# Attention's queues reordered, with two output slabs split into an idle buffer, in a two-layer decoder trunk

## The reference

```python
# layer 0
x = x + short_conv_mixer(rms_norm(x, a_norm), a_w_in, a_conv, a_w_out)
x = x + squared_relu_mlp(rms_norm(x, mlp_norm[0]), w_up[0], w_down[0])
k, v = shared_kv(x, kv_norm, w_kv, k_norm)
# layer 1: 8 heads, each with two score maps c = 0, 1 (64 features each) and 128 value features
q  = rms_norm_per_head((rms_norm(x, b_norm) @ w_q), q_norm)
for i in range(4):                                  # query blocks of 128 tokens
    sc = einsum('bqhcd,bkhcd->bhcqk', q_i, k[:128*(i+1)]) * 64**-0.5
    p  = softmax(where(causal, sc, -1e30))
    a  = p[:, :, 0] - lam * p[:, :, 1]
    o_i = einsum('bhqk,bkhe->bqhe', a, v[:128*(i+1)])
x = x + (rms_norm(o, sub_norm) * (1 - lam_init)) @ w_o
x = x + squared_relu_mlp(rms_norm(x, mlp_norm[1]), w_up[1], w_down[1])
```

## Time and profile before

| what | value |
|---|---|
| median of 3 runs | 1116.61 us (1116.53 to 1118.18) |
| the profiled execution's own time | 1118.27 us |
| its span, first to last instruction | 1116.5 us |
| busy, share of the span | PE 98%, PEld 81%, DVE 71%, ACT 43%, POOL 7% |
| mean granted TensorE clock | 0.998 of full speed |
| from the first query projection's end to the last output slab's first wait | about 631 to 758 us |

### The profile page before, as it was taken

The page is one execution under the profiler, slowest core; times in us unless marked ns, Lnnn a source line. Parts: engine busy times, 40 slices in busy tenths (PEclk is TensorE's granted clock), DMA queues, the critical chain, the costliest instruction groups (busy, mean ns, idle before and its releaser), DMA issues.

```text
span 1116.5 us, 13390 instructions
## 1 busy us (share of the span) xinstructions
PE 1097.5 (98%) x5168; PEld 904.3 (81%) x5168; DVE 788.3 (71%) x980; ACT 478.8 (43%) x695; POOL 77.4 (7%) x58
## 2 busy tenths in 40 slices
PE   8999999999999999999999998899999999999998
PEld 7888888888888888888888776677888888888887
DVE  4766554787787787688754577946668678678686
ACT  6221233453353353355532466834544344344343
POOL 0000012000000000002410211013100000000000
PEclk9999999999999999999999999999999999999999
DMA  7433462315315215201322300142323423414302
GB/s 189 104 87 108 144 203 77 114 38 172 93 39 187 76 64 163 76 1 58 113 95 76 113 1 20 58 151 86 104 75 111 116 76 117 127 59 139 87 1 76
DMA packets 144751, 105.89 MB, mean 95 GB/s; under 512 B 12592, under 2 KB 121136, under 8 KB 144688
## 3 DMA queue, kind: packets, MB, share of 16 engines
q1 hardware_dynamic: 143648, 105.03, 30.8%
q10 hardware_dynamic: 1040, 0.00, 0.1%
HBM read 102.93 MB, written 2.10 MB: 94 GB/s over the span
## 4 chain that ended last, share of the span: by engine, by line
PE 94%; DVE 3%; issue 1%; ACT 1%; DMA 1%; SPq 0%; ACTq 0%; DVEq 0%
PE ps L586 31%; PE ps L613 27%; PE ps L473 19%; PE ps L675 10%; PE ps L700 2%; PE ps L761 1%; DVE nmax L1508 1%; PE ps L739 1%; DMA kv<-in_x 1%; PE ps L751 0%; PE ps L555 0%; DVE h L1544 0%; PE ps L720 0%; PE ps L568 0%; PE ps L649 0%
## 5 line engine op out<-in xcount | busy, mean ns | idle before, releaser
L586 PE MATMUL ps<-h,w_hi 128*128 128x512 f32 x1024 | 316.2, 390 | 0.0
L613 PE MATMUL ps<-w_hi,h 128*128 128x512 f32 x896 | 277.3, 389 | 0.0
L586 PEld LDWEIGHTS ps<-h,w_hi 128*128 128x128 f32 x1024 | 191.6, 188 | 39.4
L473 PE MATMUL ps<-h,w_hi 128*128 128x512 f32 x640 | 198.6, 392 | 2.0 <-DVE h L1544 1.6
L586 PE MATMUL ps<-h,w_lo 128*128 128x512 f32 x512 | 199.3, 389 | 0.0
L613 PEld LDWEIGHTS ps<-w_hi,h 128*128 128x128 f32 x896 | 168.2, 188 | 34.8
L613 PE MATMUL ps<-w_lo,h 128*128 128x512 f32 x448 | 174.3, 389 | 0.0
L931 ACT ACTIVATE w_hi<-b_raw 128x1024 fp32r<-128x1024 f32 x80 | 82.0, 1054 | 141.4 <-PE ps L586 81.9
L473 PEld LDWEIGHTS ps<-h,w_hi 128*128 128x128 f32 x640 | 118.9, 188 | 26.8 <-DVE h L1544 1.8
L473 PE MATMUL ps<-h,w_lo 128*128 128x512 f32 x320 | 124.6, 389 | 0.0
L1245 DVE TENSOR_TENSOR w_lo<-b_raw,w_hi 128x1024 fp32r<-128x1024 f32 x80 | 95.9, 1223 | 26.7 <-ACT w_hi L931 26.7
(11 more groups left out here) (132 smaller groups left out, 1190.0 us busy)
## 6 DMA issues: line engine op xcount, KB each, us to landing
b_raw<-in_w_down SPq DMA_DIRECT2D x64, 512.0 KB, 4.5
w_raw<-in_w_up SPq DMA_DIRECT2D x64, 512.0 KB, 4.0
w_raw<-in_a_w_in SPq DMA_DIRECT2D x23, 512.0 KB, 3.7
w_raw<-in_w_kv SPq DMA_DIRECT2D x16, 512.0 KB, 3.7
w_raw<-in_a_w_out SPq DMA_DIRECT2D x8, 512.0 KB, 4.0
w_raw<-in_w_q SPq DMA_DIRECT2D x8, 512.0 KB, 3.5
w_raw<-in_w_o SPq DMA_DIRECT2D x8, 512.0 KB, 4.1
kv<-in_x SPq DMA_DIRECT2D x4, 512.0 KB, 6.9
```

Source lines behind the costliest of these rows:

```text
L473: last = nc.tensor.matmul(ps[:, bank, :], w[:, s, k * P:(k + 1) * P], src(half, k), start=(k == 0 and i == 0), stop=(k == KC - 1 and i == 2))
L586: last = nc.tensor.matmul(ps[:, v % 4, :], w[:, s_, k * P:(k + 1) * P], h_of[inp][:, half, k, :], start=(k == 0 and i == 0), stop=(k == KC ...
L613: last = nc.tensor.matmul(ps[:, CHAIN[p][tb], :], op[half][:, k, tb * P:(tb + 1) * P], w[:, s_, cols], start=(FRESH[p] and k == 0 and i == ...
```

## The change

1. **PE's order.** V(n) and V(n+1) of a head stand together in its third step, V(n+2) in its fourth and V(n+3) behind T(n+4) of the next head: V(n-1), which stood ahead of T(n), now stands behind it in a head's first step. T(n+1) has no V ahead of it any more. The last third of `project` stands behind V(n+1) and `queries_T`.
2. **DVE's order.** `out_ms` is cut into `out_sums`, which now stands ahead of M(n+3), and the rest behind it. `out_norm` stands ahead of W(n+3), and `q_stats` ahead of M(n+5).
3. **ACT's order.** E(n+4), the first of the next head, stands ahead of C(n+2). The square of `copy_o` becomes `square_o`, with a semaphore of its own, behind C(n); the copy stands behind E(n+2), ahead of C(n+1).
4. **W(n).** The exponential of c = 1 comes first, and the reciprocal waits for it alone. The product of three one-column values is a `scalar_tensor_tensor` in place of a `tensor_scalar`.
5. **Slabs 0 and 1** are split into a new buffer `wo_two`, which lies where `a_raw` lies (the MLP's buffer, idle in attention), in heads 1 and 2. Slabs 2 and 3 are split in head 7, between E(29) and C(28) on ACT and behind W(29) on DVE. Slabs 4 and 5 are split ahead of `out_hi(7)`; slabs 6 and 7 and the MLP's first two are given other places among the residual additions.
6. **The end of the projection.** `out_T(7)` stands ahead of the second half of slab 3's chunks 0 to 5.
7. **Second MLP.** The first two `copy_x` stand ahead of the split and of `row_scales`.

```diff
-WO_EARLY = {(2, 3): 0, (3, 3): 1, (4, 2): 2, (5, 2): 3}
+WO_EARLY = {1: (0,), 2: (1,), 7: (2, 3)}
-WO_SPLITS = ((4, 5), (), (6,), (7,), (), (), (8,), (), (9,))
+WO_SPLITS = ((), (), (), (6,), (7,), (8,), (), (9,), ())
...
+def freed(n):
+
+    if S_WO <= n < S_WO + 6:
+        return None if n < S_WO + 2 else used(n - 4) if n < S_WO + 4 else used(n - 8)
+    return used(n - RING) if n >= RING else None
...
+        with nc.sbuf_tensor("wo_two", [P, 2, 2, SLAB], F32R) as wo_two:
+            pass
         a_raw = sb("a_raw", [P, KC, T])
...
+        def home(n, half):
+
+            if S_WO <= n < S_WO + 2:
+                return wo_two[:, n - S_WO, half, :]
+            return (w_hi, w_lo)[half][:, slot(n), :]
...
```

PE's queue:

```diff
-            for n in range(STEPS):
-                h, i = divmod(n, 4)
-                if n + 2 < STEPS:
-                    scores(n + 2)
-                if h < 3 and i < 3:
-                    project(5 + h, (range(0, 3), range(3, 6), range(6, KC))[i])
...
-                if n:
-                    values(n - 1)
-                if i == 2 and h < 4:
-                    queries_T(4 + h)
-                if i == 3 and h:
-                    out_T(h - 1)
-                weights_T(n)
+            for h in range(H):
+                n = 4 * h
+                scores(n + 2)
+                if h < 3:
+                    project(5 + h, range(0, 3))
+                weights_T(n)
+                if n:
+                    values(n - 1)
+
+                scores(n + 3)
+                if h < 3:
+                    project(5 + h, range(3, 6))
...
+                if h >= 3:
+                    project_out(0, WO_FILL[h, 1])
+                weights_T(n + 1)
+
+                if h < H - 1:
+                    scores(n + 4)
...
+                if h == H - 1:
                     pe.wait_ge(s_exp, 2 * STEPS - 2)
                     project_out(1, range(0, 3))
...
+                values(n)
+                values(n + 1)
+                if h < 4:
+                    queries_T(4 + h)
+                if h < 3:
+                    project(5 + h, range(6, KC))
+                weights_T(n + 2)
+
+                if h < H - 1:
+                    scores(n + 5)
+                if h == H - 1:
                     project_out(1, range(3, 5))
...
+                if h:
                     out_T(h - 1)
+                values(n + 2)
+                weights_T(n + 3)
...
             project_out(2, range(2, 6))
-            project_out(3, range(0, 6))
+            project_out(3, range(0, 3))
+            out_T(H - 1)
+            project_out(3, range(3, 6))
             for m in range(ACC):
                 project_out(m, range(6, 7))
-            out_T(H - 1)
...
```

ACT's queue, in the second MLP and then in attention:

```diff
+                        if new and j == 1:
+                            copy_x(0)
+                            copy_x(1)
                         if j < 6:
                             hi(q, j + 2)
...
-                        if new and j == 1:
-                            copy_x(0)
-                        if new and j:
+                        if new and j > 1:
                             copy_x(j)
...
-                for c in range(2):
+                for c in (1, 0):
...
+            def square_o(h):
+                act.wait_ge(s_pv, 4 * h + 4)
+                if h:
+                    act.wait_ge(s_oms, h)
+                nc.scalar.activation(o_sq, ps[:, B_O, :], ACT.Square).then_inc(s_osq, 1)
...
+            for h in range(H):
+                n = 4 * h
+                exps(n + 1)
+                for m in WO_EARLY.get(h, ()):
+                    split(S_WO + m)
+                evacuate(n)
+                if h:
+                    square_o(h - 1)
+
+                exps(n + 2)
+                if h:
                     copy_o(h - 1)
...
+                evacuate(n + 1)
+
+                exps(n + 3)
+                if h < 4:
                     q_hi(4 + h)
...
+                if h < H - 1:
+                    exps(n + 4)
+                evacuate(n + 2)
+
+                if h < 3:
                     take_q(5 + h)
...
+                if h:
                     out_hi(h - 1)
...
+                evacuate(n + 3)
+            square_o(H - 1)
             copy_o(H - 1)
+            split(S_WO + 4)
+            split(S_WO + 5)
             out_hi(H - 1)
...
```

DVE's queue:

```diff
-                dve.wait_ge(s_exp, 2 * m + 2)
+                dve.wait_ge(s_exp, 2 * m + 1)
                 V.reciprocal(rinv[:, b, 0:1], rsum[:, h % 2, i, 1:2]).then_inc(s_sc, 1)
                 dve.wait_ge(s_sc, 2 * m + 1)
-                V.tensor_scalar(rinv[:, b, 1:2], rinv[:, b, 0:1], rsum[:, h % 2, i, 0:1], lams[:, 5:6],
-                                ALU.mult, ALU.mult).then_inc(s_sc, 1)
+                dve.wait_ge(s_exp, 2 * m + 2)
+                V.scalar_tensor_tensor(rinv[:, b, 1:2], rinv[:, b, 0:1], lams[:, 5:6], rsum[:, h % 2, i, 0:1],
+                                       ALU.mult, ALU.mult).then_inc(s_sc, 1)
...
+            for h in range(H):
+                n = 4 * h
+                if h >= 2:
                     out_lo(h - 2)
...
+                row_max(n + 2)
+                weights(n + 1)
+                if h < 4:
+                    q_norm_part(4 + h)
+                for m in WO_EARLY.get(h, ()):
+                    split(S_WO + m)
+
+                if h:
+                    out_sums(h - 1)
+                row_max(n + 3)
+                if h:
                     out_ms(h - 1)
...
+                weights(n + 2)
+
+                if h < H - 1:
+                    row_max(n + 4)
+                if h:
                     out_norm(h - 1)
...
+                if h < 4:
                     q_lo(4 + h)
...
+                weights(n + 3)
+
+                if h < 3:
                     q_stats(5 + h)
...
+                if h < H - 1:
+                    row_max(n + 5)
+                    weights(n + 4)
             out_lo(H - 2)
+            out_sums(H - 1)
             out_ms(H - 1)
+            split(S_WO + 4)
             out_norm(H - 1)
+            split(S_WO + 5)
             out_lo(H - 1)
```

More of the change, by code:

```diff
@@ L262, in build @@
         s_oc = sem("s_oc")
+        s_osq = sem("s_osq")
         s_ost = sem("s_ost")
@@ L471, in product @@
                         wait_chunk(k)
-                    for i, (w, half) in enumerate(((w_hi, 0), (w_hi, 1), (w_lo, 0))):
-                        last = nc.tensor.matmul(ps[:, bank, :], w[:, s, k * P:(k + 1) * P], src(half, k),
+                    for i, (w, half) in enumerate(((home(n, 0), 0), (home(n, 0), 1), (home(n, 1), 0))):
+                        last = nc.tensor.matmul(ps[:, bank, :], w[:, k * P:(k + 1) * P], src(half, k),
                                                 start=(k == 0 and i == 0), stop=(k == KC - 1 and i == 2))
@@ L758, in values @@
                 if i == 0 and h:
-                    pe.wait_ge(s_oc, 2 * h)
+                    pe.wait_ge(s_osq, h)
+                    pe.wait_ge(s_oc, h)
                 for j in range(i + 1):
@@ L840, in split @@
                 act.wait_ge(s_raw[n % RAW], 16 * (raw(n) // RAW + 1))
-                if n >= RING:
-                    act.wait_ge(s_used, used(n - RING))
-                nc.scalar.activation(w_hi[:, slot(n), :], w_raw[:, n % RAW, :], ACT.Copy).then_inc(s_whi, 1)
+                if freed(n) is not None:
+                    act.wait_ge(s_used, freed(n))
+                nc.scalar.activation(home(n, 0), w_raw[:, n % RAW, :], ACT.Copy).then_inc(s_whi, 1)
             def chunk_hi(i, m, g):
@@ L1086, in copy_o @@
                     act.wait_ge(s_oT, h)
-                    act.wait_ge(s_oms, h)
                 nc.scalar.activation(o_sb, ps[:, B_O, :], ACT.Copy).then_inc(s_oc, 1)
-                nc.scalar.activation(o_sq, ps[:, B_O, :], ACT.Square).then_inc(s_oc, 1)
             def out_hi(h):
@@ L1107, in _ @@
             q_hi(3)
-            for n in range(STEPS):
-                h, i = divmod(n, 4)
-                if n + 1 < STEPS:
-                    exps(n + 1)
-                if i == 0 and h:
+            for h in range(H):
[8 more added lines that the diff above has]
+                if h:
                     copy_o(h - 1)
-                if i == 2 and h < 4:
+                evacuate(n + 1)
+                exps(n + 3)
+                if h < 4:
                     q_hi(4 + h)
-                if i == 3 and h < 3:
+                if h < H - 1:
+                    exps(n + 4)
+                evacuate(n + 2)
+                if h < 3:
                     take_q(5 + h)
-                evacuate(n)
-                if i == 3 and h:
+                if h:
                     out_hi(h - 1)
-                if (h, i) in WO_EARLY:
-                    split(S_WO + WO_EARLY[h, i])
+                evacuate(n + 3)
+            square_o(H - 1)
             copy_o(H - 1)
+            split(S_WO + 4)
+            split(S_WO + 5)
             out_hi(H - 1)
@@ L1524, in weights, with out_sums @@
```

(6 more changed lines are left out.)

26 lines of the change are left out of this document (4 added, 22 removed).

## The result

The changed kernel takes 1103.94 us (median of 4, 1103.85 to 1104.02) against 1116.65 (median of 4, 1116.53 to 1118.18); the ratio is 0.9883, 95% interval 0.9866 to 0.99. The profiled executions are 1104.02 us round a span of 1102.2, and 1118.27 round 1116.5. Their spans differ by 14.3 us, their medians by 12.7; the first experiment says why.

The account below looks back on a forecast made before the run. DVE was taken to set the pace in heads 3 to 6, with PE waiting. The terms 0.3 + 3.9 + 6.6 - 1.0 + 2.0 + 1.2 = 13.0 us, from 1116.61, gave 1103.6 us, range 1100.0 to 1109.0.

Parts of the forecast that it names:

- heads 0 to 2: First three attention heads, bound by PE: V(n+2) no longer waits for its C, 0.3 us gained (0 to 0.9).
- head 3: Attention head 3: 10.8 us against 14.69, with a late entry of DVE, 3.9 us gained (3.0 to 5.0).
- heads 4 to 6: Attention heads 4 to 6: 25.8 us in place of 32.44, 6.6 us gained (4.5 to 7.5).
- head 7: Last attention head: slab splits on ACT delay E(30) and PE waits, 1.0 us lost (0.3 to 2.5).
- the end: Behind attention: waits for the low part of chunk 7 and a weight split go, 2.0 us gained (1.5 to 2.2).
- the second MLP: Second MLP's start: PE's wait for `copy_x` goes, 1.2 us gained (0.9 to 1.2).
- the reading of the old order: Heads 3 to 6 before: DVE's turn of 8.93 us plus a 1.2 split gives 10.15, so DVE sets the pace.
- The first rival: Chains between engines set the pace: heads 4 to 6 at 9.5 each, 1107.3 us, chance 0.15; at 10.15, 1110.2, 0.08.
- The new order: A steady head laid out anew: every input comes in time, DVE sets the pace, 8.6 us a head (8.3 to 9.3).
- W's operation: W's middle operation on DVE, four a head: 152 ns in place of 273, saving 0.48 us a head.
- DVE's turn: One head's work on DVE without a slab split: falls from 8.93 to 8.45 us.
- The clock: Rival: small waits over heads 3 to 7 make PE run at 1.2 GHz, up to 1129 us; chance 0.03.

Follow-up runs that it names:

- the first experiment: The kernel before, profiled once more with no edit: 1116.63 us, span 1114.8.
- Experiment 3: The kernel before with old orders and old W operation, but slab splits and `wo_two` as in the changed kernel: 1113.58 us, ratio 0.9971.
- experiment 5: The changed kernel with `out_T` put back behind V(n+2) on PE and `out_hi` back behind C(n+3) on ACT: 1109.07 us, ratio 0.9925.
- experiments 9 and 10: Against the changed kernel: 9 adds one more reduction a head on DVE, 1107.49 us; 10 brings back W's old `tensor_scalar`, 1104.80 us.
- Experiment 11: The changed kernel with slabs 2 and 3 split later in head 7 and `q_stats` put behind W(n+4) on DVE: 1101.66 us, ratio 0.9863.
- Experiment 6: The changed kernel with V put back one step, V(n-1) ahead of T(n) and V(n) ahead of T(n+1): 1108.52 us, ratio 0.9918.
- experiment 12: The changed kernel with the last third of `project` put back ahead of V(n), V(n+1) and `queries_T`: 1106.59 us, ratio 0.9906.
- experiment 4: The changed kernel with slabs 2 and 3 split later in head 7, behind C(30) and C(31) on ACT and W(31) on DVE: 1102.83 us.
- experiments 5 to 8: Besides 5 and 6, the changed kernel with E(n+4) back behind C(n+2) on ACT (7), 1104.51 us, or `out_sums` back behind M(n+3) on DVE (8), 1105.45 us.

## Why the prediction was right, and where its reasons were not

Its time, 1103.6 us, lies 0.3 from the measured 1103.94. Term by term, forecast and then measured between the two profiled executions: heads 0 to 2 0.3, 0.84; head 3 3.9, 3.69; heads 4 to 6 6.6, 6.43; head 7 -1.0, -1.06; the end 2.0, 2.59; the second MLP 1.2, 1.39; all 13.0, against 13.88, and 0.34 and 0.08 more lie ahead of head 0 and behind the first units: 14.3.

**Against the median two sizes are off and cancel, so the 0.3 is luck.** Head 3's 14.69 held a stretch at half clock, priced at 1.6. By experiment 1 it was worth 1.23 and chance, and absent from the executions near the median, from which the sum was then subtracted. Cleared of it the forecast is 13.0 - 1.6 = 11.4, the measured gain 12.6. The 1.2 between them are heads 0 to 2 (0.5 short), the end (0.6) and the MLP (0.2).

**The step that failed is the reading of the old order:** "With a split of 1.2 us it is the 10.15 of heads 4 and 5. So in heads 3 to 6 DVE sets the pace." The 10.15 are heads 5 and 6; head 4 had 12.13. Experiment 3 takes the split away and leaves 10.04. A loop of 10.04 set the pace, the split lay in its hole, and a turn without a bracket looked the same. The turn of 8.93 stood right behind a split, with DVE catching up, and it was read from M to M, to 728.14. The next `out_lo`, at 730.61, waits 1.03, and from `out_lo` to `out_lo` the turn is 10.03. Of the two slab splits that leave these heads the prediction says that they "are in this difference". In head 4 they were, with 2.08 in the old order; in heads 5 and 6 they were worth 0.1 until the orders changed too. The 6.6 came out (6.43) all the same, since it is a measured length minus a rightly laid out new one, and needs no reason for the old length. The first rival, chains between engines, describes the kernel before rightly, and goes wrong in its price: it let the chain survive the change. It didn't, since `out_hi` and `out_T` now stand ahead (experiment 5).

**The new order** was read rightly: laid out without holes, DVE's list has none in heads 5 and 6, and DVE's pace is confirmed by experiments 9 and 10. 8.6 was forecast for a head, 8.79, 8.62 and 8.60 came.

**W's operation** takes 220 ns, between the bounds 152 and 273: 0.05 saved each, 0.19 a head and not 0.48. The nearest row had the same instruction but no one-column scalar operand, which is the likely difference; no run separates it from the number of columns. The Trainium skill's fixed cost (VectorE: DVE Perf Modes, section on the TRN2 errata) gives 156 ns for either form, as an estimate; the trace has 220 and 273 for these and 154 for the reciprocal, so it holds for the last alone. DVE's turn was forecast at 8.45 and is 8.61: 0.28 more for W, 0.12 less, since M(n+3) now follows the small operation of the mean at once (704.15 to 704.22 us) and nothing waits for its result.

**Head 3** was put at 10.8 and took 11.00, with the forecast late entry: T(12) waits 0.59 for W(12). Experiment 11 shows that this is `q_stats`, which stands ahead of that W.

**Heads 0 to 2:** "V(n+2) no longer waits for its C" is right, without a reason given, and the size was 0.3 for 0.84. The wait hides in the busy time (13.71 of 13.78), since the records of passes overlap (one lasts 0.39 us, and the next starts 0.23 after it). By the starts it can be read. In head 1 before, V(n+2) starts 0.36 us after the mask products, as soon as C(n+2) has ended; in the changed kernel the next instruction there starts 0.12 after them:

```profile
666.08 0.48 ACT L1081 ACTIVATE work<-ps 128x384 f32<-128x384 f32 x1
666.26 0.29 PE L742 MATMUL ps<-maskb,identb 128*128 128x128 bf16 x2
666.62 0.94 PE L761 MATMUL ps<-kv,work 128*128 128x128 f32 x6
```

It is 0.22 to 0.24 in each of the three heads, 0.7 in all. Experiment 6 undoes V's order and changes nothing there; experiment 12 moves `project` and brings the wait for C back in head 0. The cover is the six passes behind `queries_T`, a part of the change that the prediction didn't price.

**Head 7** was right in place, cause and size, E(30) ending 3.67 us after E(29) (3.7) with PE waiting 1.11 (1.2); experiment 4 confirms it by taking it away. **The end:** both waits went as worked out. 2.59 came for 2.0, mostly because a bracket leaves out the time by which passes overlap. From start to start, `out_T(7)` and the next pass are 2.16 apart before and 0.35 after, which is 1.81 for the bracket of 1.56, and the wait for the weight split costs 0.55 for 0.39. The MLP's 1.39 for 1.2 is of the same kind: 1.34 from start to start for a bracket of 1.18.

**The clock** has a mean of 1.000 in the changed kernel and no slice under 9, so that rival got nothing, though small waits remained in heads 4 and 5 and one of 1.11 us in head 7.

## What to carry to other kernels

Where lists on several engines feed each other, an engine without a hole over one turn may still follow a loop: take one of its instructions away, or add one, and see whether the turn moves by that much, before pricing a gain by its busy time. And read on past a turn that has just lost its load, to the first wait behind it: here the turn ran 8.93 us, and then DVE stood still for 1.03. Work that is hidden in the hole of such a loop becomes visible when the loop goes, so a reorder and the removal of load are worth more together (12.7 us) than apart (6.3 and 3.1). Before a profiled execution's stretch goes into a sum, look whether the median has it too.

## What the hardware showed that was not expected

- A fall of the granted clock comes and goes between executions of one kernel. Before had one in head 3 in one profile and none in the other; the splits alone had one in head 7, after PE had been busy 0.71 of 2 us, and the changed kernel passed a wait of 1.11 us in the same head at 1.00, PE busy 0.89 of 2 us (722 to 724 us). Windows of 2 us in the splits alone:

```profile
728.00:730.00 2.00, 0.71 (x4) 0.47 (x4) 2.00 (x3) 2.00 (x8) 0.00 (x0) 1.00 0.09 17
...
732.00:734.00 2.00, 2.00 (x7) 1.63 (x7) 1.89 (x6) 0.46 (x2) 0.93 (x1) 0.50 1.03 303
```

- The falls go with the spread of the kernel before. Of its 25 executions timed beside the experiments, the 15 with a mean clock of 1.000 took 1116.53 to 1117.15 us, the 10 with 0.997 or 0.998 took 1117.64 to 1118.65. The 4 of the changed kernel all have 1.000 and lie within 0.17 us. So the median of the kernel before moves with the share of falls among its executions, from 1116.65 beside the result to 1117.84 beside experiments 5 to 8, and the ratios with it; the differences in this text are taken from the medians of the changed kernels, and from 1116.65.
- Instructions of one column on DVE cost by their form: 154 ns the reciprocal, 220 the `scalar_tensor_tensor` with a scalar column, 273 the `tensor_scalar` with two.
